# Block sums of the log decays: from TensorE products to VectorE differences of one running sum

## What is computed

```python
def step(s, inp):                      # _chunk_gla
    qc, kc, vc, ac = inp               # ac: log decays, all <= 0
    bcum = jnp.cumsum(ac, axis=-2)
    o_inter = jnp.einsum('bhcd,bhde->bhce', qc * jnp.exp(bcum), s)
    diff = bcum[..., :, None, :] - bcum[..., None, :, :]
    decay = jnp.where(m3, jnp.exp(jnp.where(m3, diff, 0.0)), 0.0)
    att = jnp.einsum('bhid,bhjd,bhijd->bhij', qc, kc, decay)
    o = o_inter + jnp.einsum('bhij,bhje->bhie', att, vc)
    b_last = bcum[..., -1:, :]
    s = s * jnp.exp(b_last)[..., 0, :, None] + jnp.einsum('bhcd,bhce->bhde', kc * jnp.exp(b_last - bcum), vc)
    return s, o
```

## Time and profile before

| | us |
|---|---|
| median of three runs | 1565.28 (1562.81 to 1565.93) |
| the profiled execution | 1564.52 |
| its span, first to last instruction | 1562.7 |
| TensorE busy | 1302.4 (83%) |
| VectorE busy | 663.3 (42%) |
| ScalarE busy | 425.1 (27%) |
| GpSimd busy | 503.4 (32%) |

### The profile page before, as it was taken

How to read it: one execution, slowest core, us unless ns; L and a number is a source line. 1 busy time by engine, 2 the same in 40 slices (tenths; PEclk the granted TensorE clock), 3 DMA queues, 4 the chain that set the end, 5 groups by cost and what they waited for, 6 DMA issues and landing times. The chain is left out here.

```text
span 1562.7 us, 32324 instructions
## 1 busy us (share of the span) xinstructions
PE 1302.4 (83%) x13762; PEld 995.7 (64%) x13762; DVE 663.3 (42%) x1362; ACT 425.1 (27%) x870; POOL 503.4 (32%) x423
## 2 busy tenths in 40 slices
PE   7898879999999999999999997786249979688730
PEld 6787669889889889889889876575223423233210
DVE  2659543444344354354355345452812212121137
ACT  2152223234234234234233223221012211111124
POOL 1515451371372272272263264220011111111016
PEclk9999879999999999999999998796569989899875
DMA  9958238737736836836835814801946998998955
GB/s 268 258 163 263 64 112 241 220 97 232 230 97 204 257 97 195 267 97 191 271 97 166 256 37 140 85 18 37 355 166 208 319 372 294 361 346 292 335 203 214
DMA packets 276440, 317.40 MB, mean 203 GB/s; under 512 B 17724, under 2 KB 255880, under 8 KB 274992
## 3 DMA queue, kind: packets, MB, share of 16 engines
q1 hardware_dynamic: 262232, 275.77, 57.1%
q0 software_dynamic: 8272, 22.85, 3.9%
q10 hardware_dynamic: 5792, 16.70, 3.5%
HBM read 295.94 MB, written 27.68 MB: 207 GB/s over the span
## 5 line engine op out<-in xcount | busy, mean ns | idle before, releaser
L1477 PE MATMUL psum<-arena 128*128 128x256 f32 (+3 forms) x1536 | 314.2, 359 | 3.2 <-DMA arena<-in_w_in 3.2
L1477 PEld LDWEIGHTS psum<-arena 128*128 128x128 f32 x1536 | 259.9, 196 | 33.9 <-DMA arena<-in_w_in 3.4
L2309 PE MATMUL psum<-arena 128*64 128x512 f32 (+1 forms) x832 | 181.0, 632 | 48.5 <-DMA arena<-in_exp_w 48.5
L2309 PEld LDWEIGHTS psum<-arena 128*64 128x64 f32 (+1 forms) x832 | 57.8, 140 | 154.2 <-issue 151.4
L1189 DVE COPY_PREDICATED arena<-arena,psum 128x128 f32<-128x128 int32 x280 | 84.9, 303 | 144.0 <-PE psum L1660 137.1
L1473 PE MATMUL psum<-arena 128*128 128x128 f32 x1152 | 138.2, 280 | 4.3 <-DVE arena L1057 4.3
L640 POOL TENSOR_TENSOR arena<-arena 128x768 f32<-128x768 f32 (+1 forms) x32 | 59.0, 1845 | 250.1 <-ACT arena L850 250.1
L1473 PEld LDWEIGHTS psum<-arena 128*128 128x128 f32 x1152 | 133.6, 195 | 6.9 <-issue 6.4
L1435 PE MATMUL psum<-arena 64*64 64x64 f32 x3264 | 119.8, 226 | 15.1 <-ACT arena L861 10.5
L1435 PEld LDWEIGHTS psum<-arena 64*64 64x64 f32 x3264 | 107.7, 139 | 33.1 <-issue 14.9
L1739 PE MATMUL psum<-arena 128*128 128x256 f32 x512 | 117.4, 388 | 0.8 <-ACT arena L932 0.8
(11 more groups left out here) (416 smaller groups left out, 2017.6 us busy)
## 6 DMA issues: line engine op xcount, KB each, us to landing
arena<-in_w_in SPq DMA_DIRECT2D x96, 1024.0 KB, 6.6
arena<-in_exp_w SPq DMA_DIRECT2D x96, 1024.0 KB, 12.5
arena<-in_w_out SPq DMA_DIRECT2D x32, 1024.0 KB, 6.0
arena<-in_w_in SPq DMA_DIRECT2D x24, 512.0 KB, 5.4
arena<-y_d SPq DMA_DIRECT2D x8, 1024.0 KB, 12.0
arena<-in_x_prompt ACTq DMA_DIRECT2D x15, 512.0 KB, 4.3
arena<-in_w_in SPq DMA_DIRECT2D x8, 576.0 KB, 5.2
out<-arena POOLq DMA_DIRECT2D x9, 512.0 KB, 3.0
```

Of the source, the lines that this page charges most:

```text
L1477: ins = mm(b[:, 0:n], hT[:, c, :], w[:, c, 0:n], start=(c == 0), stop=(c == KC - 1))
L2309: ins = mm(bank[2 + q % 2][at:at + width, :], xT[q % 2][:, c, at:at + width], w13[n % NB][:, c, :], start=(c == 0), stop=(c == KC - 1))
```

## The change

`sums(dt)` on TensorE forms the running sum alone: one product of 128 columns in bank 1. A new function `differences(dt)` on VectorE copies it to `E`, waits for that copy, and writes the levels as differences against the running sum at the middle of each block (six instructions and a seventh for level 6, 128 columns each). `decays(dt)` on ScalarE takes the absolute value of these 896 columns, the exponential of the running sum (128 columns), and exp(-x) of the 896. `differences(0)` stands on VectorE ahead of `scaled(0)`; `differences(dt + 1)` behind the copies of the first `lin` of group dt. The waits between `sums` and `TU` over bank 0 are gone.

```diff
@@ ScalarE
                 def decays(dt):
-                    done(act, "cum_mm", t, dt + 1, 4)
-                    if dt >= 2:
-                        done(act, "zs", t)
-                        done(act, "zks", t, dt - 1, 4)
-                    if dt == 0 and not t:
-                        done(act, "s_use", 0)
-                    for b in range(2):
-                        ins = a(E[dt % 2][0:DT_ROWS[dt], 512 * b:512 * b + 512], bank[b][0:DT_ROWS[dt], :], ACT.Exp)
-                    ins.then_inc(step("e_exp"), 1)
+                    R = slice(0, DT_ROWS[dt])
+                    done(act, "e_diff", t, dt + 1, 4)
+                    a(E[dt % 2][R, 0:896], E[dt % 2][R, 0:896], ACT.Abs).then_inc(step("e_abs"), 1)
+                    a(E[dt % 2][R, 896:1024], E[dt % 2][R, 896:1024], ACT.Exp)
+                    done(act, "e_abs", t, dt + 1, 4)
+                    a(E[dt % 2][R, 0:896], E[dt % 2][R, 0:896], ACT.Exp, scale=-1.0).then_inc(step("e_exp"), 1)
@@ VectorE
+                def differences(dt):
+                    R = slice(0, DT_ROWS[dt])
+                    done(dve, "cum_mm", t, dt + 1, 4)
+                    if dt >= 2:
+                        done(dve, "zs", t)
+                        done(dve, "zks", t, dt - 1, 4)
+                    elif not t:
+                        done(dve, "s_use", 0)
+                    e = E[dt % 2][R, :]
+                    c = e[:, 896:1024]
+                    then(cp(c, bank[1][R, 0:P]))
+                    for lvl in range(6):
+                        at = c.rearrange("p (h b i) -> p h b i", h=2, i=2 << lvl)
+                        mid = at[:, :, :, (1 << lvl) - 1:1 << lvl].to_broadcast(list(at.shape))
+                        tt(halves(e)[:, :, 64 * lvl:64 * lvl + 64].rearrange("p h (b i) -> p h b i", i=2 << lvl),
+                           at, mid, ALU.subtract)
+                    tt(e[:, 384:512], c, c[:, 63:64].to_broadcast([c.shape[0], P]), ALU.subtract).then_inc(step("e_diff"), 1)
...
+                differences(0)
                 scaled(0)
...
+                        if (pair, half) == (0, 0) and dt < 3:
+                            differences(dt + 1)
@@ TensorE
                     if dt:
                         done(pe, "e_exp", t, dt, 4)
-                    if last_level[0]:
-                        done(pe, "tU", t, last_level[0] + 1, 7)
-                    summed[0] = dt + 1
                     R = DT_ROWS[dt]
-                    C = slice(DT_COLS[dt], DT_COLS[dt] + R)
-                    for b in range(2):
-                        mm(bank[b][0:R, 0:384], la[HALF[b], C], h3(lv, P)[HALF[b], 0:6, 64 * b:64 * b + 64], start=True, stop=True)
-                    for b in range(2):
-                        ins = mm(bank[b][0:R, 384:512], la[:, C], lv[:, P * (6 + b):P * (7 + b)], start=True, stop=True)
-                    ins.then_inc(step("cum_mm"), 1)
+                    mm(bank[1][0:R, 0:P], la[:, DT_COLS[dt]:DT_COLS[dt] + R], cum, start=True, stop=True).then_inc(step("cum_mm"), 1)
...
                         if m < 6:
                             per_block(bank[3], own_block(U_b), own_block(pm)).then_inc(step("tT_mm"), 1)
-                            done(pe, "e_exp", t, summed[0], 4)
                             ins = per_block(bank[0], own_block(pm), own_block(U_b))
```

More of the change, by code:

```diff
@@ L1580, in body @@
                 unit(n, 12)
-                last_level, summed = [0], [0]
                 def sums(dt):
+                    freed(pe, "h2T_b", t)
                     freed(pe, "h2T_a", t)
-                    freed(pe, "h2T_b", t)
                     if dt:
                         done(pe, "e_exp", t, dt, 4)
-                    if last_level[0]:
-                        done(pe, "tU", t, last_level[0] + 1, 7)
-                    summed[0] = dt + 1
                     R = DT_ROWS[dt]
-                    C = slice(DT_COLS[dt], DT_COLS[dt] + R)
-                    for b in range(2):
-                        mm(bank[b][0:R, 0:384], la[HALF[b], C], h3(lv, P)[HALF[b], 0:6, 64 * b:64 * b + 64], start=True, stop=True)
-                    for b in range(2):
-                        ins = mm(bank[b][0:R, 384:512], la[:, C], lv[:, P * (6 + b):P * (7 + b)], start=True, stop=True)
-                    ins.then_inc(step("cum_mm"), 1)
+                    mm(bank[1][0:R, 0:P], la[:, DT_COLS[dt]:DT_COLS[dt] + R], cum, start=True, stop=True).then_inc(step("cum_mm"), 1)
                 sums(0)
@@ L1637, in body @@
                         ins.then_inc(step("tU_mm"), 1)
-                        last_level[0] = m
                     elif what == "unit":
```

## The result

The change makes the kernel slower, as forecast: 1605.63 us median of four runs (1602.22 to 1607.70) against 1565.61 us (1562.81 to 1566.32) for the kernel before. The ratio is 1.0257, with an interval of 1.0234 to 1.0280. The profiled execution took 1604.33 us for a span of 1602.5 us, 39.8 us more than before.

What follows compares the result with a forecast made beforehand. TensorE was taken to bound the middle tiles before the change. Added: 18 us in six middle tiles, 11 in tile 0, 9 in tile 7, 7 for the clock, 45 us over 1564.5: 1609 us, range 1590 to 1626.

Steps and rivals of the forecast that it cites:

- The chain: From one group's first lin to the next's: lin and copies, VectorE, ScalarE, GpSimd and handovers in sequence, 10.75 us a link.
- The wait ahead of lin 6: In a middle tile TensorE would stand idle some 4.4 us ahead of lin 6, waiting for GpSimd.
- At lin 8: In a middle tile TensorE would wait some 0.5 us at lin 8.
- the 1 us of waits at P4 and TU4: Between lin 6 and lin 8, about 1 us waiting for VectorE's and ScalarE's copies, queued behind the work for group 3.
- The dear ends of the range: Upper bounds for each group's small instructions, 2.4 us on VectorE and 2.3 us on ScalarE, with the clock lost: 1625 us.
- The direct gain: On TensorE, each shorter sums gives back 1.1 us: 4.5 us a tile, 36 us over eight tiles.
- lin 2's new wait: lin 2 waits 0.7 us because the copies of lin 1 now stand behind the 1.8 us of differences(1).
- Tile 0: Group 3 is ready at 207.0 instead of 196.03 us and the whole delay goes through: 11 us more.
- Tile 7: Gains and waits cancel up to lin 4; then two links take 21.5 instead of 12.64 us: 9 us more.
- The clock: TensorE at half speed for 5 to 6.8 us behind lin 6: 1 us a middle tile, 7 us in all.
- A middle tile: lin 4 comes 2.6 us earlier, lin 8 3.0 us later than before; 18 us over six tiles, without the clock's cost.
- Behind lin 8 nothing changes: The rest of a middle tile after lin 8 was said to keep its length.

Runs made afterwards that it cites:

- the dummies: Changed kernel plus products nobody reads on TensorE, five ahead of lin 1's wait and fourteen ahead of lin 6's: 1599.58 us.
- light kernel: Kernel before, with one product in each sums of tiles 1 to 7, level sums left out and decays made 1, as a measure only: 1540.49 us.
- the swap on the changed kernel: Changed kernel with the projection piece unit put ahead of lin 1 and differences of group 1 ahead of lin 0's copies: 1591.81 us.
- the differences first: Changed kernel with differences(dt + 1) on VectorE ahead of the copies of the first lin of group dt, not behind them: 1584.2 us.
- group 3 ahead: Changed kernel with group 2 prepared at lin 2 and group 3 at lin 4: 1568.08 us; group 3 at lin 5, its ScalarE work at lin 6: 1560.02 us.

## Why the prediction was right, step by step

- **The chain, the main step, held to a tenth of a us.** 10.75 us a link was said, 10.67 measured. Differences: 1.8 said, 1.82 measured (572.35 to 574.17). ScalarE: 2.05 said, 1.99 measured. GpSimd: 4.70 said, 4.67 measured. The wait ahead of lin 6: 4.4 said, 4.25 measured. At lin 8 0.5 said, 0.52 measured in this tile, 0 to 0.64 in the six. That last match is partly luck: the 1 us of waits at P4 and TU4 that was said to lie ahead of it is absent (0.13 us in this tile), since TensorE at its low clock came late to them. Where the dummies kept the clock, both are there: 0.33 and 0.80 us, and 0.63 us at lin 8. The dear ends of the range, in which each small instruction pays its full duration, are excluded (with the forecast's 1609 us they add up to 1623 us, not to 1625). By the fp32 formula in the section "The TRN2 errata" of the page "VectorE: DVE Perf Modes" of the Trainium skill one instruction of 128 fp32 columns takes 0.29 us, an estimate. The trace agrees for a single one (a mean of 283 ns over the 192 differences), but six of them take 1.30 us together, since each starts some 0.20 us after the start of the one before; the estimate of 2.3 us for the eight, made without that overlap, does not hold here.
- **The direct gain was a little too high.** 4.5 us a tile was said. The light kernel shows 2.1 us for two sums and 0.96 us for one, so some 4.1 us for four.
- **lin 2's new wait** was put at 0.7 us (its own terms, 1.8 us less 0.97 us, give 0.8). In the one tile in which the clock held, lin 1 to lin 2 takes 3.86 us instead of 3.38 us: 0.5 us.
- **Tile 0.** GpSimd is done with group 3 at 207.38 us (207.0 said), and TensorE goes on at 221.14 us instead of 210.11 us: 11.03 us, where 11 was said.

  The row of TensorE in tile 0, to the earlier trace rows:

```profile
221.14 2.83 PE L1454 MATMUL psum<-arena 64*64 64x64 f32 x48 [12.58 <-ACT arena L858]
```

  Of these, 0.84 us was there when the tile's sums(0) started, so the tile's own delay is 10.2 us, and the match to 0.03 us is luck. 1.5 us is given back behind, so the tile itself is 8.7 us longer.
- **Tile 7**: 9 us for the chain and half a us for the clock said, 9.4 us measured. TensorE, lin 6 and lin 8, to the earlier trace rows:

```profile
1067.97 1.13 PE L1667 MATMUL psum<-arena 64*64 64x64 f32 x32 [3.94 <-issue]
...
1079.10 0.69 PE L1667 MATMUL psum<-arena 64*64 64x64 f32 x32 [1.10 <-issue]
```

- **The clock: the sum was near, the place was wrong.** 1 us a middle tile was said, behind lin 6, with 5 to 6.8 us at the lower level. The clock does fall there, but for a shorter time. Single us of the changed kernel around lin 1 and lin 6 of tile 3 (busy PE, PEld, DVE, ACT, POOL; PEclk; DMA share, GB/s):

```profile
557.00:558.00 1.00, 0.00 (x0) 0.00 (x0) 0.90 (x4) 0.00 (x0) 0.00 (x0) 0.65 0.15 46
563.00:564.00 1.00, 1.00 (x19) 0.96 (x20) 0.00 (x0) 0.00 (x0) 1.00 (x2) 0.50 0.00 0
581.00:582.00 1.00, 0.96 (x36) 0.99 (x37) 0.00 (x0) 0.00 (x0) 0.00 (x0) 0.59 0.00 0
584.00:585.00 1.00, 1.00 (x15) 0.86 (x12) 1.00 (x6) 0.00 (x0) 0.00 (x0) 0.70 0.00 0
585.00:586.00 1.00, 1.00 (x7) 0.87 (x6) 1.00 (x3) 0.80 (x1) 0.00 (x0) 1.00 0.00 0
```

  Behind lin 6 it is low from 581.2 to 584.6, about 3.4 us, and the waits that TensorE would have at P4, TU4 and lin 8 take up nearly all that this costs. That step failed: I took the length of a low stretch from tile 7 for another place. The step before it failed as well: I let the clock hold behind lin 1, because it held in the one tile whose rows I read the earlier trace rows. In the kernel before it is lost there in three tiles of six, in the changed kernel in five of six, for 1.2 to 2.4 us each, here from about 557.3 to 564.1. Behind lin 6 the clock costs 0.2 to 0.4 us. At lin 1 the losses cost 1.7 us a tile as a mean (13.68 against 11.94 us from lin 0 to lin 4 where the clock held), before 0.8 us (13.40 against 12.58): 0.9 us more. Together that is near the 1 us that I had put in the wrong place, which is luck.
- **A middle tile** is 3.65 us longer, 3.0 + 1.0 was said. "Behind lin 8 nothing changes" did not hold: from lin 8 to the products behind the loop it is 0.4 us less. In all 40 us against 45: 5 us too many: 2.8 in tile 0 (11 + 0.5 said) and 2.1 in the middle tiles (24 said).

What stays open: why the 1.43 us wait ahead of lin 1 costs the clock in some tiles and not in others. In both kernels and in the light one the wait has the same length in the tiles where the clock holds and where it does not, and in four middle tiles (three with the dummies, one of the swap on the changed kernel) the clock fell there with no wait ahead.

## What to carry to other kernels

A step moved to another engine is to be priced by its place in that engine's queue: here 1.8 us of VectorE and 0.9 us more on ScalarE made lin 4 to lin 6 3.6 us longer, because they stand behind the copies of the first lin of the group before, and the closed chain across four engines is longer than TensorE's own list. Write such a chain down in full, with its handovers, and compare it with the stretch of the bound engine between its ends; if it is longer, start the step earlier rather than shorten it (1606 to 1568 us here with the same instructions). What has two states and changes between like tiles, as the clock does here, is to be read in all tiles, not in one, before a forecast rests on it.

## What the runs showed of the hardware

- **VectorE beside GpSimd.** Six 128-column fp32 differences with both inputs in SBUF take 1.30 us alone and 2.94 us beside GpSimd's products. It goes by the time that GpSimd works beside them: 1.35 us for 0.4 us of it, 1.6 us for 0.8 us, 2.0 us for 1.4 us, 2.94 us for 2.4 us (group 2 or 3 in the kernels with the differences first and with group 3 ahead), while no group without GpSimd beside it takes more than 1.31 us. One group of them, moved by a few us together with its work on ScalarE, is worth about 8 us over the kernel (1568 to 1560 us). The Trainium skill, page "SBUF — State Buffer", section "SBUF: two separate sides", describes a port pair that the two engines share under an exclusive lock; the rows agree with it. GpSimd's 768-column products keep their length, 1.82 us; its short instructions get up to 0.07 us longer (0.19 to 0.25 us for the last copy).
- **The clock falls behind short waits too**: behind 1.42 us in five middle tiles of six of the changed kernel, and behind 1.90 us in four of six of the kernel with the differences first; in tile 3 of the changed kernel a low stretch lasts 3.4 us in one place and 6.8 us in another. With the wait at lin 1 cut to 0.49 us by the piece unit it held in all six middle tiles. A filled wait is no warrant: in three middle tiles of the kernel with the dummies it fell at lin 1 with TensorE busy throughout.
- **ScalarE** takes 0.95 us for 896 fp32 columns in SBUF, and the next pass starts 0.86 us after it; a 128-column pass between the two costs 0.20 us.
